# A two-block transformer layer on one core: residual passages by token, low parts in pieces, a third gate buffer

## The reference

```python
def first_block(x, mem, ...):
    u = rmsnorm(h, norm_mix_pre); proj = u @ w_in
    ...                                    # short convolution, sparse attention
    h = h + rmsnorm(mixed @ w_out, norm_mix_post)
    hn = rmsnorm(h, norm_x_pre)
    ...                                    # cross attention on mem, 4 heads
    h = h + rmsnorm(ox @ w_o_x, norm_x_post)
    hn = rmsnorm(h, norm_ffn_pre)
    g, up = jnp.split(hn @ w_gate_up, 2, axis=-1)
    h = h + rmsnorm((jax.nn.silu(g) * up) @ w_down, norm_ffn_post)

def hybrid_layer(x, mem, ...):
    z = rmsnorm_2(x, g_mix) @ w_in
    ...                                    # mLSTM, neighbourhood attention, memory attention
    y = (gates[:, :, 0] * (h_m @ w_proj_mlstm) + gates[:, :, 1] * (h_na @ w_proj_na)
         + gates[:, :, 2] * (h_mem @ w_proj_mem))
    x = x + y @ w_out
    u = rmsnorm_2(x, g_ffn) @ w_up
    return x + jnp.square(jax.nn.relu(u)) @ w_down
```

## Time and profile before

| what | value |
|---|---|
| median of 3 runs | 1980.76 us (1980.16 to 1982.06) |
| profiled execution | 1979.19 us, span 1977.5 us |
| TensorE busy | 1789.3 us, 90% |
| VectorE, ScalarE, GpSimd busy | 36%, 34%, 37% |
| mean granted clock of TensorE | 0.927 of full speed |
| DMA | 84 GB/s on average |

### The profile page before, as it was taken

One profiled execution on the slowest core, in us unless ns is written; L12 is line 12 of the kernel. 1 busy time (PEld: TensorE's weight loads), 2 busy tenths in 40 slices (PEclk: granted clock), 3 DMA queues, 4 the chain that ended last, 5 costly groups with the idle time before them and its releaser, 6 DMA issues. The chain is left out here.

```text
span 1977.5 us, 22030 instructions
## 1 busy us (share of the span) xinstructions
PE 1789.3 (90%) x8211; PEld 1433.3 (72%) x8211; DVE 703.3 (36%) x1421; ACT 678.1 (34%) x989; POOL 722.4 (37%) x638
## 2 busy tenths in 40 slices
PE   7999969897996999999968899998978979999999
PEld 6987748676765878878847676666766768888887
DVE  6414775324315111101146164453455432222131
ACT  4113455344325233222233334332434333232231
POOL 5123203344231444554424434333313435444453
PEclk9869979898997999999978999997889989999999
DMA  4142201122121233233213223232123422232321
GB/s 156 64 128 74 66 1 65 64 86 76 64 86 43 86 106 85 86 125 99 65 43 96 85 86 103 77 89 73 49 74 112 146 64 86 86 107 85 107 86 64
DMA packets 163027, 165.14 MB, mean 84 GB/s; under 512 B 25713, under 2 KB 125160, under 8 KB 162920
## 3 DMA queue, kind: packets, MB, share of 16 engines
q1 hardware_dynamic: 140440, 147.18, 23.5%
q10 hardware_dynamic: 22480, 16.56, 2.9%
HBM read 155.33 MB, written 8.40 MB: 83 GB/s over the span
## 5 line engine op out<-in xcount | busy, mean ns | idle before, releaser
L681 POOL TENSOR_TENSOR w_low<-raw,w_high 128x512 fp32r<-128x512 f32 x513 | 673.2, 1343 | 1123.0 <-ACT w_high L792 1122.6
L1927 PE MATMUL bank<-xT_high,w_high 128*128 128x512 f32 x1016 | 419.1, 412 | 15.3 <-DVE xT_low L1299 13.1
L1928 PE MATMUL bank<-xT_low,w_high 128*128 128x512 f32 x1016 | 405.4, 399 | 0.0
L1929 PE MATMUL bank<-xT_high,w_low 128*128 128x512 f32 x1016 | 405.0, 399 | 0.0
L792 ACT CAST w_high<-raw 128x2048 fp32r<-128x2048 f32 x131 | 245.1, 1871 | 287.5 <-PE bank L1929 266.6
L1927 PEld LDWEIGHTS bank<-xT_high,w_high 128*128 128x128 f32 x1016 | 196.6, 194 | 71.9 <-issue 14.8
L1929 PEld LDWEIGHTS bank<-xT_high,w_low 128*128 128x128 f32 x1016 | 196.6, 193 | 43.3
L1928 PEld LDWEIGHTS bank<-xT_low,w_high 128*128 128x128 f32 x1016 | 197.4, 194 | 38.4
L1927 PE MATMUL bank<-w_high,hid_high 128*128 128x512 f32 x432 | 172.1, 398 | 3.7 <-POOL w_low L681 3.7
L1928 PE MATMUL bank<-w_low,hid_high 128*128 128x512 f32 x432 | 172.1, 398 | 0.0
L1929 PE MATMUL bank<-w_high,hid_low 128*128 128x512 f32 x432 | 171.9, 398 | 0.0
(11 more groups left out here) (363 smaller groups left out, 2402.1 us busy)
## 6 DMA issues: line engine op xcount, KB each, us to landing
raw<-in_w_in SPq DMA_DIRECT2D x33, 1024.0 KB, 5.2
raw<-in_w_down SPq DMA_DIRECT2D x26, 1024.0 KB, 5.0
raw<-in_w_gate_up SPq DMA_DIRECT2D x44, 512.0 KB, 5.1
raw<-in_w_up SPq DMA_DIRECT2D x16, 1024.0 KB, 5.2
raw<-in_w_kv_x SPq DMA_DIRECT2D x8, 1024.0 KB, 5.4
raw<-in_w_out SPq DMA_DIRECT2D x8, 1024.0 KB, 5.1
sg<-gate_dram ACTq DMA_DIRECT2D x8, 768.0 KB, 4.5
gate_dram<-qbuf ACTq DMA_DIRECT2D x20, 256.0 KB, 2.0
```

The source lines that it names most:

```text
L681: ins = pool.tensor_tensor(low[:, cs], full[:, cs], high[:, cs], ALU.subtract)
L1927: pe.matmul(ps, ah, bh, start=first, stop=False)
L1928: pe.matmul(ps, ah, bl, start=False, stop=False)
L1929: return pe.matmul(ps, al, bh, start=False, stop=last)
```

## The change

**Passages by token.** For ox, down2 and out2 the first two chunks run as before, the last two are taken token by token (`by_token`): chunk 2 for token j, then chunk 3 for token j, with the transposes of token j-2 between them. Sums of squares are taken for each half of 512 columns; for ox straight from the bank, so that ScalarE no longer copies it. The next product starts with three or four tiles on columns 0 to 255, which need tokens 0 and 1 alone, with the transposes of tokens 2 and 3 between them, and does columns 256 to 511 after (`first_tiles`). The norm's gain is multiplied in before the transposes, from a broadcast copy of the gain (`natural_gain`, a new load of 0.5 MB for each passage), and the high and low parts are read from the banks themselves. The first chunks of gu0, if and up0 get slots of their own (`HOMES`), outside the two in turn.

**Low parts in pieces.** GpSimd signals every piece of 512 columns; a tile's products with high weights come first, and each product with a low part waits for its own piece.

**Third gate buffer**, in two places of memory; a return is issued two steps ahead, and the casts of proj2_1 to out2 come one step earlier.

**Loads moved.** Gate biases and head gains stand before gu1, memory gains before o2, the second memory before down0.

The diff, cut to its core:

```diff
+HOMES = {"gu0": 0, "if": 0, "up0": 1}
+NATURAL = ("hf", "h2", "h4")
...
-    p.rows("ox", a["w_o_x"], 0, 2, 4)
+    p.rows("ox", a["w_o_x"], 0, 2, 4, readers="V")
...
+        c.home = HOMES.get(c.group.name) if c is c.group.chunks[0] else None
+        c.before = None
+        if c.split and c.home is None:
+            c.turn = len(ring) % HL
+            c.before = ring[-HL] if len(ring) >= HL else None
+            ring.append(c)
...
+        gnat = [at("gain_natural", 49216, [P, D]), shared[:, 0:D]]
+        homes = [(at("home_high_0", 61504, [P, CW], F32R), at("home_low_0", 69696, [P, CW], F32R)),
+                 (at("home_high_1", 8192, [P, CW], F32R), at("home_low_1", 24576, [P, CW], F32R))]
...
+        sg_third = stage[:, 1, :].rearrange("p (b s) -> p b s", b=2)
+        def sg(i):
+            if i % 3 < 2:
+                return [(sg2[:, i % 3, :, :], 0, 3)]
+            return [(sg_third, 0, 2), (shared[:, None, 2 * S:3 * S], 2, 3)]
...
-                "ox": lambda: post_gain("norm_x_post", ("h", 4)),
-                "gu0": lambda: second_memory(),
-                "gu2": lambda: post_gain("norm_ffn_post", ("h", 8)),
-                "v2": lambda: second_block_loads(),
+                "ox": lambda: (post_gain("norm_x_post", ("h", 4)), natural_gain(0, "norm_ffn_pre", pv_done, 2 * ST * PER_GROUP)),
+                "down0": lambda: second_memory(),
+                "gu2": lambda: (post_gain("norm_ffn_post", ("h", 8)),
+                                natural_gain(0, "g_mix_2", xn_ready, ntile["hf", 3] + 1)),
+                "out2": lambda: natural_gain(1, "g_ffn_2", tr_done, NT[ntile["hna", 3]][3] + 1),
+                "gu1": lambda: gate_bias_loads(),
+                "o2": lambda: memory_gains(),
...
+            def natural_gain(i, name, dead, count):
+                sp.wait_ge(dead, count)
+                sp.dma_start(gnat[i][:, :], a[name].rearrange("(o d) -> o d", o=1).broadcast_to([P, D]))\
+                    .then_inc(gnat_in, 16)
             def second_memory():
-                sp.wait_ge(x_out, 2 * XH)
+                used(sp, G["gu0"].chunks[0])
...
+                        if o + LOW < width:
+                            own.mark(ins, wl_done)
...
-                    if r >= HL:
-                        used(act, splits[r - HL])
+                    if c.before is not None:
+                        used(act, c.before)
+                    if c.group.name == "gu0" and c.home is not None:
+                        act.wait_ge(x_out, 2 * XH)
+                    if c.group.name == "up0" and c.home is not None:
+                        group_used(act, "proj2_3")
...
+                    if NT[i][0] in NATURAL:
+                        act.wait_ge(tr_done, r + 1)
+                        own.tell(act.copy(dst, TB[r % 2][:, :].rearrange("p (k t) -> p k t", k=n)), hi_done)
+                        continue
...
+                for c in g.chunks[:2]:
+                    high(c.n + 1)
+                for j in range(ST):
+                    square(j, rms[:, 56 + j:57 + j])
+                    own.link(act.activation(rms[:, 56 + j:57 + j], rms[:, 56 + j:57 + j], ACT.Identity,
+                                            bias=eps_col[:, 0:1], scale=1.0 / D))
+                for c in g.chunks[2:]:
+                    high(c.n + 1)
+                for j in range(ST):
+                    i = STATS.index((yname, j))
+                    if j == ST - 1:
+                        high(following.n + 1)
+                    square(4 + j, rms[:, i:i + 1])
+                    own.tell(act.activation(rms[:, i:i + 1], rms[:, i:i + 1], ACT.Sqrt, bias=rms[:, 56 + j:57 + j],
+                                            scale=1.0 / D), rms_done)
+                    if j:
+                        hi(ntile[hname, j - 1])
+                    residual_stat(hname, j, src_ready)
+                hi(ntile[hname, 3])
...
+            act.wait_ge(tr_done, NT[ntile["hm", 3]][3] + 1)
+            gates_back(2)
+            high(G["proj2_0"].chunks[-1].n)
             for i in range(8):
-                high(G[f"proj2_{i // 2}"].chunks[-1].n + i % 2)
-                act.wait_ge(gate_in[i % 2], 16 * (i // 2 + 1))
-                own.tell(act.activation(sg[:, i % 2, :, :], sg[:, i % 2, :, :], ACT.Sigmoid), gate_ready)
+                act.wait_ge(gate_in[i % 3], 16 * len(sg(i)) * (i // 3 + 1))
+                parts = sg(i)
+                for g, b0, b1 in parts:
+                    ins = act.activation(g, g, ACT.Sigmoid)
+                    own.link(ins) if b1 < 3 else own.tell(ins, gate_ready)
+                if i % 2 == 0:
+                    high(G[f"proj2_{i // 2}"].chunks[-1].n + 1)
                 if i:
                     act.wait_ge(y_q, i)
-                    if i < 7:
-                        gates_back(i + 1)
+                    if i < 6:
+                        gates_back(i + 2)
...
+                if phase in NATURAL:
+                    dve.wait_ge(gnat_in, 16 * (NATURAL.index(phase) + 1))
+                    own.tell(dve.scalar_tensor_tensor(out=stage[:, i % 2, :], in0=h[:, j, :], scalar=rms[:, k:k + 1],
+                                                      in1=gnat[phase == "h4"][:, :], op0=ALU.mult, op1=ALU.mult),
+                             xn_ready)
...
+            def lows(phase, j):
+                i = ntile[phase, j]
+                for b in range(NT[i][2]):
+                    r = NT[i][3] + b
+                    dst, n = turned(i, b, 1)
+                    top, _ = turned(i, b, 0)
+                    dve.wait_ge(hi_done, r + 1)
+                    own.tell(dve.tensor_tensor(dst, TB[r % 2][:, :].rearrange("p (k t) -> p k t", k=n),
+                                               top.bitcast(F32), ALU.subtract), lo_done)
...
+                def scale(t):
+                    half, j = t // 4, t % 4
+                    cs = slice(512 * half, 512 * half + 512)
+                    y = ynat[:, j, cs]
+                    dve.wait_ge(y_sq, squared + t + 1)
+                    if summed:
+                        own.link(dve.tensor_tensor(y, y, gpost[:, cs], ALU.mult))
+                    else:
+                        own.tell(dve.tensor_tensor(y, tile_in(group, t)[:, :], gpost[:, cs], ALU.mult), dense_v)
+                for t in range(ST):
+                    take(t)
+                for t in range(ST):
+                    scale(t)
+                for j in range(ST):
+                    k = STATS.index((yname, j))
+                    take(4 + j)
+                    scale(4 + j)
+                    dve.wait_ge(rms_done, k + 1)
+                    own.link(dve.reciprocal(rms[:, k:k + 1], rms[:, k:k + 1]))
+                    own.tell(dve.scalar_tensor_tensor(out=h[:, j, :], in0=ynat[:, j, :], scalar=rms[:, k:k + 1],
+                                                      in1=h[:, j, :], op0=ALU.mult, op1=ALU.add), h_ready)
+                    if j:
+                        lows(hname, j - 1)
+                    xn(hname, j, D)
+                lows(hname, 3)
+            post_halves("ox", "yx", "hf", 2, 0)
...
+            def by_token(name, xh, xl, phase, first=0, low=None, base=0):
+                c = G[name].chunks
+                for i in (0, 1):
+                    if low:
+                        pe.wait_ge(low, base + c[i].kts[-1] + 1)
+                    for k in range(first if i == 0 else 0, ST):
+                        product(c[i], k, xh, xl)
+                for j in range(ST):
+                    product(c[2], j, xh, xl)
+                    if j >= 2:
+                        turn(phase, j - 2)
+                    product(c[3], j, xh, xl)
+            def first_tiles(tiles, phase):
+                turned_ready(phase, 2)
+                for i, (c, k) in enumerate(tiles):
+                    product(c, k, xTh, xTl, part=(0, S // 2))
+                    if i < 2:
+                        turn(phase, 2 + i)
+                low_all(phase)
+                for c, k in tiles:
+                    product(c, k, xTh, xTl, part=(S // 2, S))
...
+            def low_ready(c, k):
+                need = low_before[c.n] + (1 if c.group.mode == "I" else -(-(k + 1) * c.cols // LOW))
+                if need > low_seen[0]:
+                    low_seen[0] = need
+                    pe.wait_ge(wl_done, need)
...
+                                pe.matmul(ps[:, :], xh[:, k, js], ch[:, q, :], start=first and q == 0, stop=False)
+                                pe.matmul(ps[:, :], xl[:, k, js], ch[:, q, :], start=False, stop=False)
+                            for q, k in enumerate(ks):
+                                low_ready(c, q)
+                                mm = pe.matmul(ps[:, :], xh[:, k, js], cl[:, q, :], start=False,
+                                               stop=last and q == len(ks) - 1)
+                        elif piece is None:
...
+            by_token("ox", oxTh, oxTl, "hf", first=2)
```

(3 more changed lines are left out.)

196 lines of the change are left out of this document (123 added, 73 removed).

## The result

| | before | after |
|---|---|---|
| median | 1981.01 us (1980.16 to 1982.06) | 1917.01 us (1907.26 to 1922.54, 4 executions) |
| ratio | | 0.9671, 95% interval 0.9627 to 0.9716 |
| profiled execution | 1979.19 us, span 1977.5 | 1907.26 us, span 1905.5 |
| mean granted clock | 0.927 | 0.946 |

The change makes the kernel 64 us faster by the medians. The forecast of 1906 lies 11 under the median and 1 under the profiled execution; the range of 1884 to 1936 holds all four.

A forecast was written before the change was run, and what follows sets the result against it. TensorE, busy 1789.3 of 1977.5 us, was taken as the bound, so only its idle and lower-clock time could be won. Savings of 36.2 + 29.5 + 8.9 = 74.6 us gave 1906 us, range 1884 to 1936.

The forecast's parts named there:

- Part 1: Three passages between products through a residual norm: token order and half-width first tiles save 15.6, 11.5 and 9.1, together 36.2 us.
- five falls at 1.7: Clock falls still charged to the passages: one in the first, three (5.1 us) in the second, one in the third.
- 3.0 for contention: VectorE against GpSimd in the three passages: 1.0, 1.5 and 0.5 us added to their cost.
- part 2: Nine low-part waits outside the gate stage: 19.5 us of waiting and 10 of clock won by pieces, together 29.5 us.
- part 3: Gate stage: third buffer and earlier cast remove gaps of 3.23 and 2.25 us and two clock falls, 8.9 us.
- Part 4: Loads of gains, biases and second memory moved in the queues: counted as nothing; 0 to 2.5 us gained if wrong.
- qbuf wait: TensorE waiting for VectorE to read transposed banks, 40.5 us in thirteen waits: should be gone from the list.
- A: Passages: two-input operations lose 0.95 us to GpSimd, every token is waited for; saves 18 instead of 36; 1929; chance 0.22.
- D: Slower: 382 extra low-part waits on TensorE cost time; from 0.20 us each the 74.6 is gone; chance 0.03.
- E: Nothing changes: TensorE's order is the same in effect, token-wise chunks wait for chunk 3's low; 1980; chance 0.02.
- B: All overlaps work: no contention, no stall from the clock, all 15 us of it back; 1886 us; chance 0.08.
- C: Repeated short waits hold the clock down: twelve falls in passages, none returned at nine waits; 1928 us; chance 0.05.

The follow-up runs named there:

- pieces_alone: Kernel before with only low parts signalled and waited for piece by piece, products with low parts last: 1958.81 us, ratio 0.9878.
- two_buffers: Changed kernel with two gate buffers, each return issued one step ahead, earlier casts kept: gate stage 51.3 instead of 46.2 us, one execution.
- again: The changed kernel run once more with no edit: 1905.33 us (1884.68 to 1917.18, 4 executions), ratio 0.9589.

## Why the prediction was right

**The time.** 74.6 us were forecast, 71.9 came in the profiled execution, 64 in the medians. It is a hit with two errors of opposite sign: outside the window attention 83.3, 8.7 more than said; inside it 11.3 were lost, of which the sum knew nothing. That the two meet within 1 us of the profiled execution is luck: the same program lost 8.2 less than before in that stage when it was run again, instead of 11.3 more. The medians say the same: 1981 - 83 is 1898, and 1917 and 1905 were had.

**Part 1, passages: 36.2 forecast, about 44 measured.** By the rows of after and the prediction's own way of counting (the transposes and half tiles are the forecast's, not measured apart):

| passage | forecast cost | gaps | transposes, halves | falls | measured cost | saved, forecast | saved |
|---|---|---|---|---|---|---|---|
| ox to gu0 | 11.0 | 4.4 | 4.3 | 0 | 8.7 | 15.6 | 17.9 |
| down2 to if | 21.9 | 9.3 | 4.2 | 5.1 | 18.6 | 11.5 | 14.8 |
| out2 to up0 | 8.9 | 2.0 | 4.3 | 0 | 6.3 | 9.1 | 11.7 |

The three stretches of equal work give the same: 437.0 - 391.9 = 45.1 (20.0, 14.7 and 10.4). The gaps were forecast at 4.0, 11.1 and 2.4. In the second passage they came where they were said: 2.0 on chunk 3 against 1.6, then 0.75, 1.71, 2.81 and 0.29 at the tokens against 2.3, 1.8, 2.9 and 1.9, then 1.03 and 0.72 for low parts of qk2 against 0.6. The mis-sized term is what I added for the clock: five falls at 1.7, 8.5 us. Two came, both in the second passage (962 to 966 and 993 to 1000, 10 us at the lower level, half of them lost). The 3.0 for contention did not come on top either: VectorE's slow additions are inside the gaps. These two terms, 3.4 and 3.0, and 2 us of gaps are the 8 us.

**Parts 2 and 3, low parts and gate stage: 29.5 + 8.9 = 38.4 forecast, 83.3 - 44.4 = 38.9 left.** The sum is right, the border between them was not: pieces_alone has 34.2, with 6.7 of them in the gate stage. The term of 2.25 + 1.7 us for the late cast belonged to part 2. So did the gap of 3.23, which I had read as the returned gates' and which ended with GpSimd's last low piece: part 3 had the wrong wait. In the finished kernel that buffer is worth 5 us in its stage and 1.6 in out2 (two_buffers), as long as the cast stands in front of the return. Step failed: I priced each part on the trace of before, as if the others were not there. For the pieces that hides the most: alone 34, taken out of the finished kernel 54.

**Part 4, loads moved: nothing forecast.** It was not tried alone, so whether it is worth anything is not known.

**Predicted signs.** Gaps of at most 3 us in the passages: yes, 2.81 the longest, in the second passage and before its first half tile. The qbuf wait "gone from the list": no, 11.4 is left, outside the passages. No wait for pieces over 3 us: yes, 1.2, and the late one at "out" is now for the cast itself, 3.58 us. Nothing over 1 us in the gate stage: yes. The stall of 2.9 at ox's last chunk: 2.1.

**The rivals.** A, the chains stay on the path (1929): its mechanism is in the trace, but at six of the twenty additions and norms of the three passages, 3.3 us of VectorE together, not at every token. D, the waits are not free: refuted by pieces_alone, which gains with them. E: refuted by the table. B, no contention and no stall from the clock (1886): it asks for 94.4 us outside the window attention by its own terms (one of which, 9.8 for the clock, is 8.5 by the five falls counted), and 83.3 came; that again had 1884.7 once is the short window attention of that execution. C, the clock held down (1928): in the passages no; but a clock held down is what separates 1907 and 1922 from 1885, in a stage where I had not looked, because its rows in before (85.8 of 90.3 us busy) looked like nothing could be won or lost. I listed the time at the lower clock in what can be won (289 us by the mean of 0.927: 0.073 x 2 x 1977.5), and took its price only at the edited places.

**What stays open:** what decides the level in the window attention; whether the changed kernel needs its third buffer once the casts stand where they did; and the value of the token order in the whole time, which the spread covers.

## What to carry to other kernels

Split the first tiles of the next product by tokens before reordering the last product by tokens: the work put in front of the last tokens was worth twice the order here. Where one engine both casts and asks for the next transfer, ask first. Late pieces, passages and buffers are each other's cover, so price a part with the others in place, or name the part without which the rest is lost. A stage of small matmuls can be shown fully busy at the lower clock; compare its granted clock over several executions before crediting a change with what it does, and try one spare matmul per step where it varies.
